# Sampled tokens' attention in products of fp16 halves, joins spread by one group, and an earlier first load of the mixed columns in a hybrid decoder layer

## What is computed

```python
def hybrid_layer(h, W, l, past):
    u = rmsnorm(h, W['norm_mix_g'][l])
    proj = u @ W['w_in'][l]
    qa, ka, va, qc, kc, vc, z, xbc, dt_raw = jnp.split(proj, offs, axis=-1)
    # A: window of 128 keys, 4 heads on 2 kv heads, with sinks; past: 128 cached keys per sequence
    oa, _ = gathered_window_attention(qa, past[0], past[1], ka, va, WIN_A, 1, tab_a, W['a_sinks'][l])
    # C: (window, dilation) = (128, 1), (512, 4), (2048, 16), 4 heads; past: the 2048 last keys
    for window, dil in C_BRANCHES:
        o, s = gathered_window_attention(qc, past[2], past[3], kc, vc, window, dil, tab_c, None)
    oc = jnp.einsum('nlhbd,nlhb->nlhd', jnp.stack(outs, axis=-2), wts)
    # B: conv, silu, state-space scan in chunks of 128 tokens, gated norm -> ob
    h = h + jnp.concatenate([oa, ob, oc], axis=-1) @ W['w_out'][l]
    h = h + jnp.square(jax.nn.relu(rmsnorm(h, W['norm_mlp_g'][l]) @ W['w_up'][l])) @ W['w_down'][l]
```

## Time and profile before

| | |
|---|---|
| median of 3 runs | 2873.24 us (2868.71 to 2873.33) |
| the profiled execution | 2873.65 us, its span from first to last instruction 2871.4 us |
| PE busy | 2623.0 us, 91% of the span |
| DVE, ACT, POOL busy | 1102.7, 819.9, 269.2 us (38%, 29%, 9%) |
| mean granted TensorE clock | 0.942 of 2.4 GHz |
| chain that ended last | 70% PE, 6% DVE, 3% ACT |
| dense matmuls of line 2344 in that chain | 56% of the span |

### The profile page before, as it was taken

One profiled execution on the slowest core, in us unless ns is written; L12 is line 12 of the kernel. 1 busy time (PEld: TensorE's weight loads), 2 busy tenths in 40 slices (PEclk: granted clock), 3 DMA queues, 4 the chain that ended last, 5 costly groups with the idle time before them and its releaser, 6 DMA issues.

```text
span 2871.4 us, 42038 instructions
## 1 busy us (share of the span) xinstructions
PE 2623.0 (91%) x17098; PEld 1580.7 (55%) x17098; DVE 1102.7 (38%) x2685; ACT 819.9 (29%) x1522; POOL 269.2 (9%) x300
## 2 busy tenths in 40 slices
PE   7799558999878999899899999998999999899999
PEld 4455334465434655444455554444656545688887
DVE  4345325456624656641333344204334521222222
ACT  4332205465434543331322120114321201211111
POOL 0011101111101211000111110001111000000000
PEclk9899759999989999999989999999999999999999
DMA  6335325555454656665343445433434334222222
GB/s 216 107 130 168 106 96 200 186 174 165 144 181 155 206 181 190 202 225 190 112 123 106 119 123 140 137 128 109 145 118 139 114 111 157 89 96 96 92 95 85
DMA packets 342655, 405.99 MB, mean 141 GB/s; under 512 B 62975, under 2 KB 273919, under 8 KB 342208
## 3 DMA queue, kind: packets, MB, share of 16 engines
q1 hardware_dynamic: 342464, 403.31, 43.9%
HBM read 296.01 MB, written 107.23 MB: 140 GB/s over the span
## 4 chain that ended last, share of the span: by engine, by line
PE 70%; DVE 6%; ACT 3%; issue 2%; DMA 2%; SPq 2%; POOL 0%; POOLq 0%; DVEq 0%; ACTq 0%
PE core_dense L2344 56%; PE core_spare L2461 2%; PE core_spare L2449 2%; PE core_spare L2567 1%; DMA core_js<-scratch_sums 1%; PE core_spare L2437 1%; PE core_spare L2603 1%; PE core_dense L2369 1%; PE core_spare L2472 1%; PE core_spare L2502 1%; DVE core_col L2136 1%; DVE core_h L2041 1%; PE core_spare L2524 1%; DMA core_ring<-scratch_kept_w 1%; PE core_spare L2538 0%
## 5 line engine op out<-in xcount | busy, mean ns | idle before, releaser
L2344 PE MATMUL core_dense<-core_u,core_ring 128*128 128x512 f16 (+2 forms) x4800 | 891.3, 346 | 18.7 <-DVE core_u L2014 16.9
L2344 PEld LDWEIGHTS core_dense<-core_u,core_ring 128*128 128x128 f16 x4800 | 474.3, 99 | 399.9 <-issue 53.9
L2344 PE MATMUL core_dense<-core_r_hi,core_ring 128*128 128x512 f16 (+2 forms) x2560 | 665.8, 346 | 2.5 <-DVE core_h L2041 2.5
L2344 PE MATMUL core_dense<-core_r_lo,core_ring 128*128 128x512 f16 (+2 forms) x1280 | 443.4, 346 | 0.0
L2344 PEld LDWEIGHTS core_dense<-core_r_hi,core_ring 128*128 128x128 f16 x2560 | 255.1, 100 | 209.1 <-issue 25.7
L2041 DVE SCALAR_TENSOR_TENSOR core_h<-core_dense,core_h 128x512 f32<-128x512 f32 (+2 forms) x160 | 94.5, 591 | 539.6 <-PE core_dense L2344 539.5
L2344 PE MATMUL core_dense<-core_pu,core_ring 128*128 128x512 f16 x1152 | 270.5, 393 | 29.3 <-DMA core_pu<-scratch_u 23.1
L1863 ACT ACTIVATE core_r<-core_dense 128x512 f32<-128x512 f32 (+2 forms) x160 | 82.8, 517 | 653.4 <-PE core_dense L2344 653.4
L2029 DVE TENSOR_TENSOR core_r<-core_r 128x512 f32<-128x512 f32 (+2 forms) x160 | 94.9, 593 | 400.5 <-ACT core_r L1863 400.3
L2344 PEld LDWEIGHTS core_dense<-core_pu,core_ring 128*128 128x128 f16 x1152 | 115.9, 101 | 164.5 <-issue 23.8
L564 PE MATMUL tok_prod<-tok_w_hi,tok_u 128*128 128x512 f16 (+1 forms) x768 | 204.6, 356 | 0.0
(11 more groups left out here) (319 smaller groups left out, 2767.1 us busy)
## 6 DMA issues: line engine op xcount, KB each, us to landing
core_ring<-scratch_kept_w SPq DMA_DIRECT2D x264, 512.0 KB, 3.9
scratch_kept_w<-core_ring SPq DMA_DIRECT2D x72, 512.0 KB, 5.2
core_qkv<-out_tok SPq DMA_DIRECT2D x48, 384.0 KB, 5.3
core_piece<-in_w_up SPq DMA_DIRECT2D x32, 512.0 KB, 4.5
core_piece<-in_w_down SPq DMA_DIRECT2D x32, 512.0 KB, 4.3
out_tok<-tok_tok SPq DMA_DIRECT2D x16, 644.0 KB, 3.0
core_piece<-in_c_kt SPq DMA_DIRECT2D x32, 288.0 KB, 3.9
core_piece<-in_c_v SPq DMA_DIRECT2D x16, 576.0 KB, 4.3
```

What stands on the lines that cost most here:

```text
L2344: ins = pe.matmul(bank, w[:, k, part, :], s, start=first and j == 0, stop=last and j == 2, skip_group_check=True)
```

## The change

Three things change in `core`.

**Halves.** Every cached piece is split into two fp16 halves as it arrives: a new unit `split` (32 of them) has ACT copy `piece` to `halves[:, 0]` and DVE subtract to `halves[:, 1]`, of 1280 or 1152 columns. Queries, probabilities and new values are kept as halves too (`qs`, `pt`, `pnt`, `vn`). Each fp32 matmul of `sk`, `sv`, `se` and of the scores between new tokens becomes three fp16 matmuls (`both`). `piece` becomes one buffer, loaded when the piece before it is split. The splits stand at slots 3, 6, 9, ... (`sk` moves to 5, 8, 11, ...) in block 1 and at slots 8, 10, 12, ... (`sv` moves to 9, 11, 13, ...) in block 2. Raw weights go through `staged`, which lies where `piece` and `halves` are used later.

**Joins.** In blocks 1 to 3 an empty slot stands between a join's weights and its turn, so that two dense groups lie between one turn and the next. In the first stage the gap from the scan's part 0 to part 1 is 2 half groups for 3, and so the joins come four half groups earlier.

**First mix load.** The four column groups of the scan (2 to 5) are loaded once the third turn is stored, the others once the fourth is, ahead of the raw tiles' fetches. The `x` loads of block 0, and the store of `p_conv`, move from the fourth turn to behind the last `silu`.

```diff
-        piece = a.sb("piece", [P, RW, 10 * P])
-        w_raw = [piece[:, i, 0:8 * P].rearrange("p (k c) -> p k c", c=P) for i in range(RW)]
+        with ExitStack() as early:
+            staged = early.enter_context(nc.sbuf_tensor("core_staged", [P, RW, 10 * P], F32))
+        w_raw = [staged[:, i, 0:8 * P].rearrange("p (k c) -> p k c", c=P) for i in range(RW)]
+        piece = a.sb("piece", [P, 10 * P])
+        with ExitStack() as early:
+            soft = early.enter_context(nc.sbuf_tensor("core_soft", [P, 10 * P], F32))
+        halves = a.sb("halves", [P, 2, 10 * P], F16)
...
             for c in range(4):
-                for part, gap in zip(scan_parts(c), (3, 1, 1)):
+                for part, gap in zip(scan_parts(c), (2, 1, 1)):
...
-                    some += [[j[0]], [j[1], j[2]], [j[3], j[4]], [j[5], j[6]], [j[7]]]
+                    some += [[j[0]], [], [j[1], j[2]], [], [j[3], j[4]], [], [j[5], j[6]], [], [j[7]]]
...
                         for k in range(16):
-                            some[4 + 3 * k] = some[4 + 3 * k] + [("sk", k // 2, k % 2, 0)]
+                            some[3 + 3 * k] = some[3 + 3 * k] + [("split", k, 0, 0)]
+                            some[5 + 3 * k] = some[5 + 3 * k] + [("sk", k // 2, k % 2, 0)]
...
                         for k in range(16):
-                            some[8 + 2 * k] = some[8 + 2 * k] + [("sv", k // 2, k % 2, 0)]
+                            some[8 + 2 * k] = some[8 + 2 * k] + [("split", 16 + k, 0, 0)]
+                            some[9 + 2 * k] = some[9 + 2 * k] + [("sv", k // 2, k % 2, 0)]
...
                 def load_mix(b):
-                    if b == 0:
-                        sp.wait_ge(col_done, 36)
-                    sp.wait_ge(m_out, 16 * 2 * 4 * (b + 1))
+                    if b:
+                        sp.wait_ge(m_out, 16 * 2 * 4 * (b + 1))
                     sp.wait_ge(j_out, 16 * 4 * 4 * (b + 1))
...
+                            sp.dma_start(u[:, i, 0:2, 0:w], mix_of[i][:, 0:2, s:s + w]).then_inc(mix_in, 16)
+                            sp.dma_start(u[:, i, 6:8, 0:w], mix_of[i][:, 6:8, s:s + w]).then_inc(mix_in, 16)
+
+                def load_scanned():
+
+                    sp.wait_ge(col_done, 36)
+                    sp.wait_ge(m_out, 16 * 2 * 4)
+                    for i in range(2):
+                        sp.dma_start(u[:, i, 2:6, 0:512], mix_of[i][:, 2:6, 0:512]).then_inc(mix_in, 16)
...
                 def load_keys(n, j):
-                    if n:
-                        sp.wait_ge(smp_done, 2 * n + j - 1)
-                    elif j == 0:
+                    if n or j:
+                        sp.wait_ge(piece_lo, 2 * n + j)
+                    else:
                         sp.wait_ge(smp_turned, TURN_Q)
...
-                    if kind == "col" and (b, i, k) == (3, 11, 1):
+                    if n and units[n - 1][0:2] == ("turn", 2):
+                        load_scanned()
+                    if n and units[n - 1][0:2] == ("turn", 3):
                         load_mix(0)
...
-                    elif kind == "turn" and b == 3:
+                    elif kind == "silu" and b == 3 and i == 2:
                         sp.wait_ge(conv_done, KT * 4)
                         sp.dma_start(io["p_conv"], halo[:, :, :]).then_inc(conv_out, 16)
                         for j in range(XR):
...
+                    elif kind == "split":
+                        w = (10 - part % 2) * P
+                        act.wait_ge(piece_in, arrived[part])
+                        act.wait_ge(smp_done, part)
+                        if part == 16:
+                            act.wait_ge(smp_turned, TURN_P)
+                        act.activation(halves[:, 0, 0:w], piece[:, 0:w], ACT.Copy).then_inc(piece_hi, 1)
...
+                    elif kind == "split":
+                        w = (10 - n % 2) * P
+                        dve.wait_ge(piece_hi, n + 1)
+                        dve.tensor_tensor(halves[:, 1, 0:w], piece[:, 0:w], halves[:, 0, 0:w], ALU.subtract).then_inc(piece_lo, 1)
...
+                def both(out, left, right, first=True, last=True):
+
+                    for m, (l, q) in enumerate(((0, 0), (0, 1), (1, 0))):
+                        ins = pe.matmul(out, left(l), right(q), start=first and m == 0, stop=last and m == 2, skip_group_check=True)
+                    return ins
...
-                                last = pe.matmul(spare[5 - s][:, at:at + w], piece[rows, j, k * P:(k + 1) * P], qs[rows, 2 + j, q0:q0 + w], start=True, stop=True)
+                                last = both(spare[5 - s][:, at:at + w], lambda l: halves[rows, l, k * P:(k + 1) * P], lambda l: qs[rows, l, 2 + j, q0:q0 + w])
```

More of the change, by code:

```diff
@@ L1994, in _ @@
                         turn(b)
-                    elif kind in ("sq", "sx", "se"):
+                    elif kind in ("sq", "split", "sx", "se"):
                         sampled(kind, b)
@@ L2558, in sampled @@
                                     at = 12 + DEC_T * q
-                                    pe.matmul(spare[5 - s][:, at:at + DEC_T], piece[rows, j, KC * P:], qs[rows, q, DEC_T * n:DEC_T * n + DEC_T], start=True, stop=True)
+                                    both(spare[5 - s][:, at:at + DEC_T], lambda l: halves[rows, l, KC * P:], lambda l: qs[rows, l, q, DEC_T * n:DEC_T * n + DEC_T])
                         for k in range(KC):
@@ L2602, in sampled @@
                             q0 = DEC_T * n + t0
-                            last = pe.matmul(out[:, :, t0:t0 + w], piece[:, j, k * P:(k + 1) * P], st[:, s0:s0 + 2, q0:q0 + w],
-                                             start=k == 0, stop=k == KC - 1, skip_group_check=True)
+                            last = both(out[:, :, t0:t0 + w], lambda l: halves[:, l, k * P:(k + 1) * P], lambda l: pt[:, l, s0:s0 + 2, q0:q0 + w], k == 0, k == KC - 1)
                         last.then_inc(smp_done, 1)
```

125 lines of the change are left out of this document (71 added, 54 removed).

## The result

The changed kernel takes 2773.07 us (median of 4 runs, 2767.82 to 2774.77) against 2873.07 us, a ratio of 0.9659 with a 95% interval of 0.9645 to 0.9672: 100 us, or 3.4%, faster. The forecast was 2799 with a range of 2768 to 2838; the gain is a third larger than the 74 us forecast, and the time is 5 us above the lower end of the range. The profiled execution took 2767.82 us, with a span of 2766.0.

A forecast was written before the change was run, and what follows sets the result against it. PE, busy 91% of 2871.4 us, was taken as the bound, through its own time, waits and clock. From 2873.65 us, -28.5 - 23 - 22.6 - 6.3 + 4 + 2 = -74.4 gave 2799 us, range 2768 to 2838.

The forecast's parts named there:

- products: matmul time: In sk and sv units, 1416 fp16 matmuls at 30.4 ns take 43.0 us for 71.5: -28.5 us, from -37 to +69.
- clock, splits, SP, bank waits around them: Clock of the sk and sv stretches, -23 us (0 to -34); splits, SP's waits and sv's bank wait, +2 us (0 to 48).
- joins: PE's waits at turns in blocks 1 to 3 go, the first stage's stay: -22.6 us.
- mix load: First out group waits some 14 us, ended by an x load, and not 20.11: -6.3 us.
- scan gap: First stage's scan, two half groups for three: waits of 3.2 and 0.5 us where 0.6 and 0 stood, +4 us (0 to 10).
- the nearest has 65: Price of small fp16 matmuls taken from a row with 65 moving columns and a weight load each: 30.4 ns, low end 24.
- weight load sets the pace: Rival, chance 0.03: at line 2590 unhidden weight loads make small matmuls 99 ns each, 2920 us; decides from 67 ns on.
- Four or five falls: Clock falls that stay around sk units, at 1.7 us in the dense group and some 0.5 in the unit, 10 us.
- the four slots that were named: Slots 5, 8 and 11 of block 1, behind a tile's probabilities, and slot 29, behind a scan's first part, keep clock falls.
- the 34 us of the two stretches: Clock loss against 0.98 in the sk and sv stretches, 28 and 6 us, taken as the whole excess.
- the weights, five tiles ahead: SP's loads behind its waits for splits: weights are five tiles ahead; part of the +2 us (0 to 48).
- best case of 2780: Rival, chance 0.13: all clock falls go and small matmuls take 24 ns, -34 and -37 us for -23 and -28.5.

The follow-up runs named there:

- e4: The kernel before with joins spaced, scan gap of 2 and the new mix load, but sampled products in fp32 at their old places: 2834.93 us.
- e1: The changed kernel with only the joins put back close, one dense group less between weights and turn in the hosted stretches of blocks 0 to 2: 2808.76 us.
- e10: The kernel before with only the new mix load in two parts, x loads and p_conv one finished unit earlier; gap of 3, joins close, fp32 products: 2867.26 us.
- e2: The changed kernel with the first stage's scan gap of 3 again, the first mix load still in two parts: 2765.80 us.
- e3: The changed kernel with key products in another order, all nine of the first 64 rows, then all nine of the others, not in turn: 2779.08 us.
- e8: The changed kernel with each key unit ahead of the hosted attention or scan unit of its slot instead of behind it: 2762.95 us.
- e7: The changed kernel with the 33 loads of the biases in four parts, one behind each of four dense groups: 2760.19 us.

## Why the prediction was right, and where its sizes were off

| term | forecast, us | measured, us |
|---|---|---|
| products: matmul time | -28.5 | -45.9 (timeline) |
| clock, splits, SP, bank waits around them | -21 | -16 (e4: 61.9 less 45.9) |
| joins | -22.6 | -35.7 (e1) |
| mix load | -6.3 | -6.1 (e10's timeline; -4.9 by medians) |
| scan gap | +4 | +5.1 (e2's timeline; +7.3 by medians) |
| sum | -74.4 | -98.6 by the values named first, -95.2 by medians, of 100.0 |

**The small matmuls.** The forecast took 30.4 ns, the row with 65 columns, and let 24 be the low end. Value products take 26.7, key products 14.1. The step that failed is "the nearest has 65": it was near in its weight load but not in its rows. The key products lie on 64 rows, in turn on one half and the other and in turn in two banks, and e3 shows that this turn is what brings 24 to 25 ns down to 14. The sign stood in the rows read: 36 records of fp32 key products took 2.11 us and 18 records of fp32 value products on 128 rows 2.01, 59 and 112 ns, and that factor of 1.9 was not carried to the fp16 price. Of the 17.4 us that the term missed, keys are 15.7. The rival "weight load sets the pace", at 99 ns and with a decision point of 67, was far off. The Trainium skill (TensorE: Matmul & The Clock Gate, Back-to-back issue gap) gives 81 ns per load and matmul at 128 columns, and no unit here, with 1 to 16, comes near that. The Trainium skill's least spacing of about 25 ns, in the same section, roughly fits the 24.4, 25.0 and 26.7 ns of the products that don't alternate, and not the 14.1 of those that do; the measurement decides.

**The clock.** The direction was right, and as far as can be told the size: 0.97 and 1.00 in the forecast stretches, where 0.95 and 0.97 had been asked for. The -16 of the table is a net. PE's wait for the ring is 7.9 us in e4 and 15.5 in the changed kernel, and 1.0 us of waits for `halves` is new; without these 8.6 us the clock and the rest come to about -25, an estimate from these rows, against -23. Four or five falls were to stay behind bank waits, and five did (named under e4; 24 dense matmuls take 7.77 us behind the unit at 1419.14), but only three of them in the four slots that were named: slot 11 has none, and slots 17 and 20 have one each. e8, which takes the waits away, brings the stretch to 0.99. What was missed is that the joins had a low clock of their own, 0.90 in [1165, 1215]. So the 34 us of the two stretches were not the whole excess, as the forecast said, and 0.98 was not the most that could be reached.

**Joins.** The waits of blocks 1 to 3 went as forecast, and no excess came back on DVE. But the term counted only waits, 22.6; undoing it costs 35.7, 25.3 of it waits. The groups behind a wait, where the clock is low, had to be priced with it. That is the second term that was too small.

**First stage.** The forecast of the wait (14 us, ended by `x`) against 15.1 measured, the gain of 6.3 against 6.1 and the loss of 4 against 5.1 all hold. The 4 does not follow from its own rows, though: waits of 3.2 and 0.5 us for 0.6 and 0, each twice, are 6.2 us more. Measured were 3.3, 2.0, 0.6 and 0.6, 5.3 more than before. That the figure taken lies near the loss is luck. Net the stage is worth about nothing, and a gap of 3 would have kept the 5 to 7 us of e2.

**Splits, SP and banks.** A split takes 1.3 us on ACT and 1.5 on DVE, as forecast, and PE waits for the splits themselves 1.0 us (on `core_halves` in 2 places of the trace after). SP's wait for a split was named, and put at 2 us together with the rest. With the halves PE's wait for the ring grew by 7.6 us (e4 against the changed kernel), nearly all of it at the one place where a long row of loads stands behind a split. The 13.0 us of e7 are the price of that whole row, which the kernel before had too with a wait of 1.6. The forecast's cover, "the weights, five tiles ahead", ends where SP issues nothing for the ring for 32 us.

So the direction and the mechanisms were right, and the sizes of the clock, the mix load and the gap. The products were short by 17.4 us and the joins by 13.1, both the same way, and the splits and SP cost some 7 us more than the 2 put for them. The time came 26 us below the forecast and 7 below its best case of 2780. It is inside the range only by the margin left below that case, for which no row was given, and that much of it is luck.

## What to carry to other kernels

Price a wait on PE together with the clock of the groups behind it: the joins' 25 us of waits were worth 36 here. Ahead of replacing fp32 products by three fp16 ones, read the pace of the fp32 products by their row count: here the 64-row products that alternate ran at 1.9 times the pace of the 128-row ones in fp32 and again in fp16, and with three times as many matmuls all of them together took 25.6 us for 71.5. When a queue issues many small loads in a row, count the time between two fetches of what the busiest engine eats (32 us for a ring of five tiles here), and spread the loads; and ahead of narrowing one gap, ask whether the wait behind it is measured from a fixed time or from the end of the work that you delay.

## What the runs showed of the hardware

- Fp16 matmuls with 1 to 4 moving columns, each with its own 128-column weight load, pass at 14 ns each when they alternate, by threes, between the two 64-row halves and two output banks, and at 24 to 25 ns when they don't (e3); on 128 rows, with 2 to 16 columns, at 26.7 ns. In fp32 the same two kinds took 59 and 112 ns for each of the two records of a matmul.
- Behind fp16 units of 0.7 to 1.0 us no dense group is slow unless a wait of 2 to 3 us stood ahead of the unit, and then it is (five of five in the key stretch). Behind fp32 units of 2.1 us that waited for nothing most groups beside the key units are slow (7.04 us for 24 matmuls that take 5.34), and some are not (5.35 us at 1814.59 in the kernel before).
- The changed kernel reaches its first `col` group at 417.9 us in one profile and at 422.0 in another, and the first ends 6.1 us earlier. In the profiles of all kernels of this case the mark lies at 417.7 to 418.4 or at 421.4 to 422.7, with nothing between.
